# Sample attention with the spread rows copied by ScalarE, feed-forward layers joined into one block, and norms rebuilt

## The reference

```
# layer 0: RWKV-7 time mixing, whose end is a group norm per head of 64
y = (y - mean) * rsqrt(var + GN_EPS) * lnx_w + lnx_b
out = ((y + bonus) * g) @ w_o ;  h = h + out
# after each layer's mixing: feed-forward layer with a causal convolution of width 3
xn = rms_norm(h, g_norm);  u = xn @ w_up;  gp = xn @ w_gate          # 1024 -> 2816
h  = h + (silu(conv3(gp)) * u) @ w_down                              # 2816 -> 1024
# between the layers: keys and values for layer 1
kv = rms_norm(h, kv_norm) @ w_kv                                     # 1024 -> 3 * 512
# layer 1: sparse attention, its queries from the same h
q  = rms_norm(rms_norm(h, ln_mix1) @ wq, qnorm) / 8
# sample part of it: for each sequence 4096 past keys in pages, normed per key
s  = (q . k) * rsqrt(mean(k*k) + EPS) + distance penalty + block mask
p  = exp(s - max(s));  out = (p @ v) / sum(p)
```

## Time and profile before

| | |
|---|---|
| median of 3 runs | 3016.11 us (3015.32 to 3017.39) |
| profiled execution, its own time | 3014.09 us |
| span in its trace, first to last instruction | 3012.3 us |
| PE busy | 2562.3 us, 85% |
| DVE busy | 1412.0 us, 47% |
| ACT busy | 831.1 us, 28% |
| POOL busy | 788.3 us, 26% |
| mean granted TensorE clock | 0.915 |

### The profile page before, as it was taken

The page is one execution under the profiler, slowest core; times in us unless marked ns, Lnnn a source line. Parts: engine busy times, 40 slices in busy tenths (PEclk is TensorE's granted clock), DMA queues, the critical chain, the costliest instruction groups (busy, mean ns, idle before and its releaser), DMA issues. The chain is left out here.

```text
span 3012.3 us, 61936 instructions
## 1 busy us (share of the span) xinstructions
PE 2562.3 (85%) x25248; PEld 2024.8 (67%) x25248; DVE 1412.0 (47%) x2862; ACT 831.1 (28%) x1881; POOL 788.3 (26%) x480
## 2 busy tenths in 40 slices
PE   5998999838699979597998878878888876999798
PEld 3776999616699979444443655545555554999798
DVE  6208565341477710102334246657667743577600
ACT  2215334130222221001111135545545521122210
POOL 0001000100476633000000049921111100667541
PEclk8999999769799989797999879989989988999999
DMA  2121001101222221316883100035444521222231
GB/s 93 56 65 39 4 4 32 51 14 56 65 84 84 77 99 57 138 56 243 306 294 112 45 15 2 1 135 182 164 161 162 178 70 44 84 82 80 70 106 60
DMA packets 107842, 276.22 MB, mean 92 GB/s; under 512 B 13353, under 2 KB 14250, under 8 KB 105450
## 3 DMA queue, kind: packets, MB, share of 16 engines
q1 hardware_dynamic: 107626, 273.18, 27.0%
HBM read 264.42 MB, written 16.97 MB: 93 GB/s over the span
## 5 line engine op out<-in xcount | busy, mean ns | idle before, releaser
L334 PE MATMUL ps<-parts 128*128 128x288 f32 x6336 | 847.0, 296 | 87.6 <-POOL parts L303 87.6
L334 PEld LDWEIGHTS ps<-parts 128*128 128x128 f32 x6336 | 846.1, 189 | 88.3 <-issue 88.3
L303 POOL TENSOR_TENSOR parts<-kept,parts 128x1024 fp32r<-128x1024 f32 (+1 forms) x120 | 314.8, 2625 | 180.2 <-ACT parts L298 173.3
L308 POOL TENSOR_TENSOR parts<-kept 128x1024 fp32r<-128x1024 f32 x88 | 179.3, 2037 | 461.5 <-DMA kept<-in_wall 304.3
L1660 PE MATMUL ps<-mix,kept 128*128 128x512 f32 (+1 forms) x544 | 227.8, 579 | 0.0
L1342 DVE TENSOR_TENSOR kept<-kept,ps 128x576 f32 x32 | 24.2, 756 | 421.4 <-PE ps L334 294.3
L2080 POOL TENSOR_SCALAR mix<-kept 128x896 f32<-128x896 f32 x16 | 40.4, 2524 | 573.1 <-SPq L2070 573.1
L1660 PEld LDWEIGHTS ps<-mix,kept 128*128 128x128 f32 x544 | 101.3, 194 | 120.0 <-issue 120.0
L2543 POOL TENSOR_TENSOR mix<-mix 128x512 f32<-128x512 f32 x64 | 66.7, 1042 | 394.7 <-DVE mix L2246 368.0
L2094 POOL TENSOR_SCALAR mix<-mix 128x128 f32<-128x128 f32 (+3 forms) x128 | 136.3, 1084 | 23.6 <-DVE mix L2055 23.6
L1453 DVE TENSOR_SCALAR kept<-kept 128x512 f32<-128x512 f32 x44 | 72.2, 1641 | 125.4 <-ACT kept L1430 125.4
(11 more groups left out here) (426 smaller groups left out, 4829.0 us busy)
## 6 DMA issues: line engine op xcount, KB each, us to landing
mix<-in_cmp_pool SPq DMA_DIRECT2D x256, 256.0 KB, 4.9
mix<-in_slc_pool SPq DMA_DIRECT2D x192, 256.0 KB, 3.4
kept<-in_wall SPq DMA_DIRECT2D x88, 512.0 KB, 3.6
mix<-in_wall SPq DMA_DIRECT2D x48, 512.0 KB, 3.6
kept<-in_wdown SPq DMA_DIRECT2D x32, 704.0 KB, 4.0
kept<-in_slc_pool SPq DMA_DIRECT2D x64, 256.0 KB, 3.4
out_s_win<-in_state_win SPq DMA_DIRECT2D x1, 8064.0 KB
mix<-in_wkv SPq DMA_DIRECT2D x1, 6144.0 KB, 17.2
```

What stands on the lines that cost most here:

```text
L303: return e.tensor_tensor(low.bitcast(F32R), whole, high, ALU.subtract)
L308: e.tensor_tensor(high.bitcast(F32R), whole, c.c("one").to_broadcast([P, whole.shape[1]]), ALU.mult).then_inc(*steps.step())
L334: mm = pe.matmul(out, l[:, f, :].bitcast(F32R), m[:, first + f, a:b].bitcast(F32R), start=first + f == 0 and k == 0, stop=last and f == n ...
```

## The change

In the group norm, mids get four buffers and the gained tile buffers of its own (`fin`); ScalarE's roots move one turn later than its squares, VectorE's `scaled` and `gated` likewise. In the feed-forward layer, norm, up/gate and down projection share one block: weight loads and GpSimd's splits can begin beside the norm, the first two weight blocks are multiplied tile by tile as the norm delivers them, and the down projection's loads, splits and products follow the last turn without a border; its loop over turns is written out. The norm's scratch tiles are four convolution buffers, since the weight rings occupy the old place; the convolution state to be stored lies in `rs`. The key/value norm moves into `kv_side`, where the weights come in 8 loads. The norm before the query is gone: `query` multiplies h by the row `rs` that the key/value norm left (both norms are of the same h), and `compress` uses another buffer. In the sample attention ScalarE copies the spread rows, as the first thing in its tick, TensorE makes spreads before means, and `inv` has two buffers instead of three.

The diff, cut:

```
@@ rw_output
-    mid, sq, root, root2 = two(0), two(2), two(4), two(6)
+    mid, sq, fin = some(MEM["A"], 4), some(MEM["A"] + 4 * NT, 2), some(MEM["A"] + 6 * NT, 2)
+    root, root2 = some(MEM["K"], 2), some(MEM["K"] + 2 * NT, 2)
...
-            for f in range(FT + 2):
+            for f in range(FT + 3):
                 if f < FT:
                     centre(f)
-                if 0 <= f - 1 < FT:
-                    scaled(f - 1)
                 if 0 <= f - 2 < FT:
-                    gated(f - 2)
+                    scaled(f - 2)
+                if 0 <= f - 3 < FT:
+                    gated(f - 3)
...
                     if f >= 2:
-                        act.wait_ge(*V.at(seg, f"out{f - 2}"))
-                    act.activation(sq[f % 2], mid[f % 2], ACT.Square).then_inc(*A.step(f"sq{f}"))
-                    act.wait_ge(*T.at(seg, f"var{f}"))
...
+                        act.wait_ge(*T.at(seg, f"var{f - 2}"))
+                    act.activation(sq[f % 2], mid[f % 4], ACT.Square).then_inc(*A.step(f"sq{f}"))
+                if 0 <= f - 1 < FT:
+                    m = f - 1
...
@@ ffn
+FFN.put("high1", W8).put("low1", W8).put("high0", W8).put("low0", W8)
+DOWN_AT = [FFN["high0"]] + [FFN["x"] + _k * SLOT for _k in range(3)]
+DOWN_RAW = [MEM["x"] + _k * HALF_FF * P for _k in range(2)]
+UNITS = [(0, 0), (1, 0), (0, 1), (1, 1)] + [(_m, _h) for _m in range(2, FT) for _h in range(2)]
...
+            sp.wait_ge(*G.at(seg, "split3", last))
+            for u, (m, k) in enumerate(UNITS):
+                if u == 1:
+                    sp.wait_ge(*V.at(seg, "parted0", last))
+                if u >= 2:
+                    sp.wait_ge(*G.at(down, f"rest{u - 2}"))
+                sp.dma_start(raw[u % 2], d["wdown"][m + layer * FT, :, k * HALF_FF * P:(k + 1) * HALF_FF * P]).then_inc(
+                    down_got[u % 2].sem, 16)
...
+            for j in range(2):
+                pe.wait_ge(*G.at(seg, f"split{j}"))
+            for f in range(FT):
+                pe.wait_ge(*V.at(norm, f"low{f}"))
+                for j in range(2):
+                    for o, a, b in BANKS:
+                        for k, (l, m) in enumerate(((0, 0), (0, 1), (1, 0))):
+                            mm = pe.matmul(c.ps[j][:, o:o + b - a], w[j][l][:, f].bitcast(F32R),
+                                           x[m][:, f, a:b].bitcast(F32R), start=f == 0 and k == 0,
+                                           stop=f == FT - 1 and k == 2)
+                    if f == FT - 1:
+                        mm.then_inc(*T.step(f"mm{j}"))
...
-            with pe.Fori(0, turns) as i:
+            with pe.Fori(1, turns) as i:
...
+            for u, (m, k) in enumerate(UNITS):
+                pe.wait_ge(*G.at(down, f"rest{u}"))
...
+                else:
+                    pe.wait_ge(*V.at(seg, "parted1", last))
+                for o, a, b in BANKS:
+                    mm = product(pe, c.ps[m % 4][:, o:o + b - a], dw[u % 4], F, k * HALF_FF, k == 1, a, b)
+                mm.then_inc(*T.step(f"mm{u}"))
...
+            for u in range(len(UNITS)):
+                if u < 2:
+                    g.wait_ge(down_got[u].sem, 16)
+                    g.wait_ge(*T.at(seg, f"mm{2 + u}", last))
+                    split(c, g, G, raw[u], *map(flat, dw[u])).then_inc(*G.step(f"rest{u}"))
+                else:
+                    g.wait_ge(*A.at(down, f"rounded{u}"))
+                    rest(g, raw[u % 2], *map(flat, dw[u % 4])).then_inc(*G.step(f"rest{u}"))
...
@@ kv_side
-            sp.dma_start(c.v(KVM["w"], FT * 1536), d["wkv"]).then_inc(*got.more())
+            for f in range(FT):
+                sp.dma_start(c.v(KVM["w"] + f * 1536, 1536), d["wkv"][:, f * 1536:(f + 1) * 1536]).then_inc(*got[f].more())
...
                     for f in range(FT):
+                        if n == 0:
+                            pe.wait_ge(*V.at("kv", f"normed{f}"))
+                            pe.wait_ge(*got[f].all())
                         mm = pe.matmul(o, x[:, f, t * P:t * P + m], w[:, f, br, :], start=f == 0, stop=f == FT - 1)
...
@@ query
+            for f in range(FT):
+                v.scalar_tensor_tensor(out=x[:, f], in0=h[:, f], scalar=c.col("ln_mix1", f), in1=rs, op0=ALU.mult,
+                                       op1=ALU.mult).then_inc(*V.step(f"normed{f}"))
...
@@ sample_attention, VectorE
-                    v.wait_ge(*T.at(seg, f"rb{n}"))
-                    if n >= 2:
-                        v.wait_ge(*T.at(seg, f"turn{n - 2}"))
-                    v.tensor_copy(x, spread).then_inc(*V.step(f"spread{n}"))
                     v.wait_ge(*T.at(seg, f"raw{n}"))
-                    v.wait_ge(*V.own())
+                    v.wait_ge(*A.at(seg, f"spread{n}"))
                     v.tensor_tensor(x, x, raw[n % 2], ALU.mult).then_inc(*V.step(f"t{n}"))
...
@@ sample_attention, ScalarE
             for t, i, k in ticks():
+                if 0 <= t - 1 < last:
+                    n = t - 1
+                    act.wait_ge(*T.at(seg, f"rb{n}"))
+                    if n >= 2:
+                        act.wait_ge(*T.at(seg, f"turn{n - 2}"))
+                    act.activation(probs[n % 2], spread, ACT.Copy).then_inc(*A.step(f"spread{n}"))
                 if 0 <= t + 1 < last:
                     n = t + 1
-                    r = inv[n % 3]
+                    r = inv[n % 2]
...
@@ sample_attention, TensorE
             for t, i, k in ticks():
+                if 0 <= t - 1 < last:
+                    spreads(pe, t - 1)
                 if 0 <= t + 1 < last:
                     means(pe, t + 1)
-                if 0 <= t - 1 < last:
-                    spreads(pe, t - 1)
                 if 0 <= t < last:
                     scores(pe, t)
...
@@ write_program
         with c.memory("mix1"):
-            rms_norm(c, "norm_kv", MEM["h"], MEM["x"], "kv_norm")
             kv_side(c)
             compress(c)
-            rms_norm(c, "norm_mix1", MEM["h"], MEM["x"], "ln_mix1")
             query(c)
```

More of the change, by code:

```diff
@@ L1271, in _ @@
             V.end(turns)
[L1274 to L1309, removed]
-                    rest(g, ring[u % 2], flat(w[u][0]), flat(w[u][1])).then_inc(*G.step(f"rest{u}"))
-            G.end(turns)
-        @block.tensor
-        def _(pe):
-            with pe.Fori(0, turns) as i:
-                T.begin(seg, i)
-                for u in units:
-                    pe.wait_ge(*G.at(seg, f"rest{u}", i))
-                    if u % 2 == 0:
-                        pe.wait_ge(*V.at(seg, f"done{u // 2}", i, back=1))
-                    for o, a, b in BANKS:
-                        mm = product(pe, c.ps[u // 2][:, o:o + b - a], w[u], F, u % 2 * half, u % 2 == 1, a, b)
-                    mm.then_inc(*T.step(f"mm{u}"))
-            T.end(turns)
-        @block.vector
-        def _(v):
-            with v.Fori(0, turns) as i:
-                V.begin(seg, i)
-                for j in range(2):
-                    v.wait_ge(*T.at(seg, f"mm{2 * j + 1}", i))
-                    add(v, i * 2 + j, banks(c.ps[j])).then_inc(*V.step(f"done{j}"))
-            V.end(turns)
@@ L1382, in _ @@
         def _(sp):
-            sp.dma_start(whole[:, 0:CONV[0]], d["conv"][layer]).then_inc(*state.more())
+            sp.dma_start(conv_in[:, :], d["conv"][layer]).then_inc(*state.more())
             with sp.Fori(0, turns) as i:
@@ L1395, in _ @@
         def _(pe):
-            with pe.Fori(0, turns) as i:
+            T.begin(norm)
+            for f, k in pairs:
+                pe.wait_ge(*V.at(norm, f"pair{f}"))
+                for a, b in ((0, SEQ), (SEQ, NT)):
+                    mm = pe.matmul(c.ps[3][:, a:b], c.c("mean"), tmp[k][:, a:b], start=f == 6, stop=f == 4)
+                mm.then_inc(*T.step(f"mean{f}"))
+            T.end()
+            T.begin(seg, 0)
+            for j in range(2):
[10 more added lines that the diff above has]
+                        mm.then_inc(*T.step(f"mm{j}"))
+            for j in range(2, 4):
+                pe.wait_ge(*G.at(seg, f"split{j}"))
+                for o, a, b in BANKS:
+                    mm = product(pe, c.ps[j][:, o:o + b - a], w[j % 2], x, 0, True, a, b)
+                mm.then_inc(*T.step(f"mm{j}"))
+            with pe.Fori(1, turns) as i:
                 T.begin(seg, i)
@@ L1472, in _ @@
                     v.wait_ge(*V.own())
-                    split(c, v, V, gc[k], tile(F[0]), tile(F[1])).then_inc(*V.step())
+                    split(c, v, V, gc[k], tile(F[0]), tile(F[1])).then_inc(*V.step(f"parted{k}"))
             V.end(turns)
-    ffn_down(c, layer, F)
+            V.begin(down)
+            for u, (m, k) in enumerate(UNITS):
+                if k == 1:
+                    v.wait_ge(*T.at(down, f"mm{u}"))
+                    v.tensor_tensor(halves(h[:, m]), halves(h[:, m]), banks(c.ps[m % 4]), ALU.add).then_inc(
+                        *V.step(f"added{m}"))
+            V.end()
 ATT = Map(STAGE)
@@ L1514, in _ @@
             T.begin("kv")
-            pe.wait_ge(*got.all())
```

(5 more changed lines are left out.)

217 lines of the change are left out of this document (156 added, 61 removed).

## The result

The changed kernel takes 2830.48 us (median of 4 runs, 2828.35 to 2834.04) against 3016.2: ratio 0.9385, 95% interval 0.9369 to 0.9401. The forecast was 2836 us.

| stage | before | after | difference | forecast |
|---|---|---|---|---|
| all ahead of the group norm (unchanged) | 597.8 | 601.4 | +3.6 | 0 |
| group norm | 81.8 | 41.6 | -40.2 | -39 |
| feed-forward, layer 0 (norm, up/gate, down) | 477.4 | 454.0 | -23.4 | -29 |
| feed-forward, layer 1 | 476.7 | 454.3 | -22.4 | -29 |
| key/value side | 164.4 | 140.1 | -24.3 | -22.7 |

A forecast was written before the change was run, and what follows sets the result against it. TensorE was busiest, with idle stretches at stage borders and closed loops between engines in sample attention. Gains of 39 + 22 + 36 + 22.7 + 19.7 + 41 = 180 us from 3014.1 gave 2834, as median 2836 us; range 2808 to 2862.

The forecast's parts named there:

- Group norm: Group norm of layer 0: three tiles in flight, VectorE the bound, 41 to 42 us against 81.4, -39 us.
- First turn: Feed-forward layers: loads and splits beside the norm start TensorE 16.6 us sooner; net 10.7 a layer, -22 us for two.
- The hole: Feed-forward, before block three: its split, 4.4 us, no longer hidden behind block two; lower clock at restart, about 1.5 us.
- Joint: Up/gate to down projection: early loads and GpSimd passes leave TensorE 1 us of waiting; 18 a layer, -36 us.
- Key/value side and query: Key/value weights load beside the norm, -22.7 us; the whole norm before the query goes, -19.7 us.
- Sample attention: Sample attention: copy moved to ScalarE, spreads before means; 51.7 us a sample, 6.1 less than 57.8; -41 us.
- light tick: Sample-attention tick not lengthened by VectorE: 5.1 us, 0.2 slower than before, because `values` waits for ScalarE's `o` copy.
- heavy ticks: Sample-attention ticks that VectorE lengthens: with a copy less, tick 1 takes 9.2 us, ticks 2 to 5 21.0.
- (1): Sample attention: new `o` loop and ScalarE's longer queue eat what heavy ticks give back; 2877 us, chance 14%.
- (2): Feed-forward layers: GpSimd and VectorE block each other, halving both terms, 29 us less gain; 2865 us, chance 9%.
- (3): Sample attention: `o` never late, ticks 2 to 8 at TensorE's own pace, 4.3 us; 2799 us, chance 6%.
- (4): Sample attention: ScalarE's queue becomes one serial chain per tick, 8.1 to 9.2 us, slower than before; 3093 us, chance 3%.

## Why the prediction held, point by point

**Group norm.** Right in mechanism and size: 41.6 us against 41 to 42, with VectorE as the bound.

**First turn.** The mechanism was right, the prices of GpSimd and of the clock were too low. I let two Newton steps meet a pass, for 2.5 us; three did, and cost 1.60 + 2.03 + 2.77 - (0.76 + 0.46 + 0.76) = 4.4 us. The durations without a pass are those of the key/value norm of the same trace, which has none:

```profile
1176.89 0.76 DVE L1664 TENSOR_TENSOR kept<-kept 128x576 f32<-128x576 f32 x1
1177.68 0.46 DVE L1666 TENSOR_SCALAR kept<-kept 128x576 f32<-128x576 f32 x1
1178.18 0.76 DVE L1668 TENSOR_TENSOR kept<-kept 128x576 f32<-128x576 f32 x1
```

The passes began 7.6 us after the norm's start, not some 5, and lay over all three. TensorE started 19.86 us after the norm's start instead of 17.8. The hole was 3.65 us against 4.4, but the slow clock behind it cost about 2.8 us against 1.5. So the term was -8 a layer (34.5 before, less 19.9, 3.65 and 2.8), not -10.7.

The Trainium skill's Advanced Engine Details and Errata (section VectorE Performance Modes) says that GpSimd instructions and VectorE instructions in two-port modes block each other; its table gives such a mode to tensor_scalar and none to tensor_tensor. The trace agrees for the tensor_scalar step, which took 2.03 us instead of 0.46. The two tensor_tensor steps were held as well, for which the Trainium skill's page cited in the prediction has the wider condition, two SBUF inputs. The trace gives the size: the wait lasts to the end of the running pass, in this norm up to 2.0 us.

**Joint.** The gap of 18 us fell to 2.15, not to 1: the last split ended 8.3 us before TensorE's last up/gate product instead of 8.8, the load took 4.2 us instead of 4.0, and the two passes 2.53 + 3.57 = 6.1 instead of 5.7. What I counted wrongly are the 2 us of slow clock that were to vanish. They stayed, for behind the 2.15 us of waiting the clock fell too:

```profile
1022.57:1033.13 10.56, 10.55 (x66) 10.32 (x66) 8.94 (x13) 2.07 (x2) 5.81 (x2) 0.84 0.38 137
1033.53:1042.00 8.47, 8.47 (x64) 8.47 (x65) 0.56 (x1) 1.42 (x2) 6.64 (x2) 1.00 0.54 172
```

The first unit's 66 matmuls took 10.56 us at a mean clock of 0.84; at 1.00, as right behind, 66 take 8.7. The term was -15.7 a layer, not -18.

**Key/value side and query.** Right: first product 13.9 us after the stage's start against 14.7. The query's term lies between -19 and -23, since the same stages took 307.3 to 311.2 us in the other twelve executions of the changed form.

**Sample attention.** The light tick is 5.08 us against 5.1, set by `values` behind `o`; tick 1 is 9.2 in the mean, as forecast; ticks 2 to 5 take 20.5 against 21.0, tick 0 5.9 against 6.2. A middle sample takes 50.7 us instead of 51.7; six of them gain 42.3 us instead of 36.6, the first and last together 8.3 instead of 4.4. Together -50.6 instead of -41: a term sized too low.

The reason that I gave for the heavy ticks was right only in part. I priced them by the copies that VectorE loses, tick 1 too. For ticks 2 to 5 that holds: the copy alone takes them from 27.1 to 22.6. But the order alone, with every copy left on VectorE, takes them to 22.3, and tick 1 falls with the order (to 9.6) and not with the copy (10.9). TensorE's order, to which I gave no share of this gain, brings most of the term by itself.

That the total came within 6 us of the forecast is luck: the 10 us by which this term was too low make up for most of the 12 by which the feed-forward terms were too high.

**The rivals.** The ticks did not stay (1). GpSimd and VectorE do block each other (2), but the feed-forward terms fell short by a fifth, 12 of 58 us. Of these 6 us a layer about 2 are the blocking in the norm; about 3 are the lower clock, 1.3 more than charged behind the hole and 1.8 at the joint. That `o` is never late (3) is refuted by the wait at `values`; with `o` made early, light ticks do fall to 3.2 to 4.5 us, around the 4.3 that rival 3 gave, and ticks 1 and 5 then decide. ScalarE's serial chain (4) did not form: in the light tick shown the roots wait 0.44 us, for means alone.

## What to carry to other kernels

Where no engine is full, write down each closed loop of waits through the engines' queues and time it; the longest one is the tick, and a loop that is opened is worth only the distance to the next. So try the second-longest wait together with the first: here two edits that took 17.0 and 11.5 us off a stage took 54.2 together. A small copy that another engine waits for belongs at the front of its engine's turn, ahead of work that nobody is waiting for.

## What the runs showed of the hardware

A VectorE instruction whose operands all lie in SBUF did not run beside a GpSimd pass: in the norm it finished 0.3 to 0.6 us after the pass ended (1.60, 2.03 and 2.77 us instead of 0.76, 0.46 and 0.76), and a pass that met such an instruction took longer too (2.40 instead of 1.89). One that reads PSUM was not held (0.76). The whole trace of the changed kernel bears this out: 158 VectorE instructions with all operands in SBUF started while a pass over weights (L308 or L303 of GpSimd) had more than 0.1 us to run, and every one ended after the pass; all 42 with an operand in PSUM ended before it.

And TensorE paid for a short wait twice here: behind gaps of 2.15 and 3.65 us the granted clock was at its lower level, 1.2 GHz, for a while, which cost about 1.8 and 2.8 us more; behind one of 0.50 us it stayed at 2.4 GHz.
